# The head's modulation: weights in whole rows, transpositions for one-column products, small tables on GpSimd's queue

## What is computed

```python
cond = jax.nn.silu(c)
for layer in range(DEPTH):
    mod = cond @ ada_w[layer] + ada_b[layer]
    sh_m, sc_m, gt_m, sh_f, sc_f, gt_f = jnp.split(mod, 6, axis=-1)
    h = modulate(rms_norm(x, norm_mix[layer]), sh_m, sc_m)
    ...
# modulate(hn, shift, scale) = hn * (1 + scale) + shift
```

## Time and profile before

| | us |
|---|---|
| median of 3 timed runs | 2018.76 |
| lowest and highest of them | 2018.72 and 2019.66 |
| the profiled execution | 2013.86 |
| its span, first to last instruction | 2012.0 |
| TensorE busy in it | 1691.6 |
| VectorE busy | 606.6 |
| ScalarE busy | 361.9 |
| GpSimd busy | 74.2 |

### The profile page before, as it was taken

The page is one execution under the profiler, slowest core; times in us unless marked ns, Lnnn a source line. Parts: engine busy times, 40 slices in busy tenths (PEclk is TensorE's granted clock), DMA queues, the critical chain, the costliest instruction groups (busy, mean ns, idle before and its releaser), DMA issues.

```text
span 2012.0 us, 26580 instructions
## 1 busy us (share of the span) xinstructions
PE 1691.6 (84%) x11294; PEld 1049.1 (52%) x11294; DVE 606.6 (30%) x1546; ACT 361.9 (18%) x817; POOL 74.2 (4%) x80
## 2 busy tenths in 40 slices
PE   6997879976777667999987776787799998999988
PEld 4756754533333333755544333353378874568753
DVE  1657633211111112662320111111141053311292
ACT  1113213100000001322311100010121223211271
POOL 0000100000000001000000000000100000000000
PEclk9997998988788889999888888898899999999899
DMA  9995326999999999773699999999983343066100
GB/s 352 377 310 209 85 85 255 419 428 428 428 428 429 428 428 409 268 269 123 265 426 422 427 430 428 424 427 428 421 291 139 130 168 115 1 189 201 53 1 32
DMA packets 142766, 582.33 MB, mean 289 GB/s; under 512 B 30940, under 2 KB 42332, under 8 KB 117984
## 3 DMA queue, kind: packets, MB, share of 16 engines
q1 hardware_dynamic: 113504, 558.49, 69.3%
q10 hardware_dynamic: 24000, 10.32, 2.0%
q0 software_dynamic: 5184, 12.43, 1.8%
HBM read 571.41 MB, written 13.11 MB: 291 GB/s over the span
## 4 chain that ended last, share of the span: by engine, by line
PE 50%; DMA 35%; DVE 8%; issue 2%; ACT 2%; PEld 1%; PEldq 1%; SPq 0%; DVEq 0%; ACTq 0%; POOL 0%; POOLq 0%
DMA ring<-in_exp_w_dram 31%; PE bank L735 15%; PE bank L724 6%; PE bank L872 6%; PE bank L2133 5%; PE bank L2497 3%; PE bank L2194 2%; PE bank L2487 2%; DMA ring<-in_hawk_w_mem_kv_dram 1%; PE bank L2139 1%; DMA ring<-in_ada_w_dram 1%; DMA taken_rows<-expert_out,route_rows 1%; PE bank L1999 1%; DVE pair_probs L3273 1%; DVE pair_probs L3258 1%
## 5 line engine op out<-in xcount | busy, mean ns | idle before, releaser
L2133 PE MATMUL bank<-ring,hidden_room 128*32 128x512 f32 x2032 | 291.5, 697 | 165.8 <-DMA ring<-in_exp_w_dram 163.4
L735 PE MATMUL bank<-hT,ring 128*128 128x256 f32 x1344 | 294.0, 381 | 2.6 <-ACTq L167 2.2
L735 PEld LDWEIGHTS bank<-hT,ring 128*128 128x128 f32 x1344 | 256.6, 191 | 39.1 <-issue 2.8
L2133 PEld LDWEIGHTS bank<-ring,hidden_room 128*32 128x32 f32 x2032 | 66.2, 121 | 318.9 <-DMA ring<-in_exp_w_dram 175.8
L2194 PE MATMUL bank<-ring,hidden_room 128*32 128x256 f32 x1984 | 162.4, 481 | 46.7 <-DMA ring<-in_exp_w_dram 30.9
L2394 DVE COPY hidden_room<-bank 128x512 f32<-128x512 f32 x64 | 44.3, 691 | 513.0 <-PE bank L2133 513.0
L2139 PEld LDWEIGHTS bank<-kc,hidden_room 128*128 128x128 f32 x1024 | 133.9, 204 | 73.0 <-issue 65.5
L2139 PE MATMUL bank<-kc,hidden_room 128*128 128x32 f32 x1024 | 141.3, 284 | 3.0 <-DVE hidden_room L2394 1.6
L2194 PEld LDWEIGHTS bank<-ring,hidden_room 128*32 128x32 f32 x1984 | 75.4, 131 | 100.8 <-issue 68.1
L2301 ACT COPY hidden_room<-bank 128x512 f32<-128x512 f32 x64 | 37.5, 586 | 474.8 <-PE bank L2133 474.8
L724 PE MATMUL bank<-ring,hT 128*128 128x512 f32 (+2 forms) x288 | 114.3, 557 | 0.0
(11 more groups left out here) (588 smaller groups left out, 1845.9 us busy)
## 6 DMA issues: line engine op xcount, KB each, us to landing
ring<-in_exp_w_dram SPq DMA_DIRECT2D x189, 2048.0 KB, 26.6
ring<-in_ada_w_dram SPq DMA_DIRECT2D x24, 2048.0 KB, 16.8
ring<-in_hawk_w_in_dram SPq DMA_DIRECT2D x15, 2048.0 KB, 9.2
ring<-in_even_w_in_dram SPq DMA_DIRECT2D x7, 2048.0 KB
ring<-in_gla_w_in_dram SPq DMA_DIRECT2D x6, 2048.0 KB, 20.2
ring<-in_nsa_w_in_dram SPq DMA_DIRECT2D x5, 2048.0 KB, 8.2
ring<-in_even_w_out_dram SPq DMA_DIRECT2D x2, 2048.0 KB
expert_out<-kc POOLq DMA_DIRECT2D x8, 512.0 KB, 9.2
```

What stands on the lines that cost most here:

```text
L735: last = nc.tensor.matmul(pair[m // 2][0:rows, (m % 2) * T:(m % 2 + 1) * T], w[:, k, m * P:m * P + rows], src[:, k, :], start=(k == 0), st ...
L2133: last = nc.tensor.matmul(dst[quarters[k % NQ], :], own[:, q, k % 2, k // 2, :], w[:, k, :], start=(k < NQ), stop=(k >= KD - NQ))
```

## The change

Chunks 0 to 3 keep their 2 MB but are cut the other way: chunk q now holds two blocks of 128 rows of ada_w and all 2048 columns, so that a partition reads two runs of 8 KB. With that each chunk adds to all four banks (condition_rows), and the sums are ready only after the fourth. turn_tiles moves behind the fourth chunk. The one-column products give way to four times four transpositions of 128 columns (turn_row_parts), after which VectorE adds the four partial sums with a reduction for each bank. ScalarE copies two banks, VectorE the two others. The 14 small tables are issued by GpSimd at the start of the stage in place of ScalarE. The loads of c, x, first_gain and ada_bias by ScalarE stay as they are and in their order. The last keep_warm has four products in place of three and waits for the first reduction.

```diff
@@ chunk list
-                for j in range(4):
-                    ada_chunk(0, j)
+                for q in range(4):
+                    cols_of(A["ada_w"][0], 2 * q, 2, [(0, 2048)])
@@ new functions
+        def condition_rows(c, q, dsts, cond):
             for j in range(4):
+                for n in range(2):
+                    g = 2 * ((j + q) % 2) + n
+                    last = nc.tensor.matmul(dsts[j][32 * g:32 * g + 32, :], cond[:, 2 * q + n, :], slot(c)[:, n, 512 * j:512 * (j + 1)],
+                                            start=(q < 2), stop=(2 <= q))
+            return last
...
+        def turn_row_parts(dst, parts, j):
+            for m in range(4):
+                last = nc.tensor.transpose(dst[:, m * P:(m + 1) * P], parts[:, j, m * P:(m + 1) * P], ident)
             return last
@@ ScalarE
-                        for stage_rows, table in ((rowsB, COL_B), (rowsA, COL_A)):
-                            for name, (at, n) in table.items():
-                                act.dma_start(stage_rows[at:at + n, :], flat(A[name]).rearrange("(r p) -> r p", p=P)).then_inc(tables_in.up(16), 16)
-                        for j in range(4):
-                            act.wait_ge(chunk_used.sem, used0 + j + 1)
+                        act.wait_ge(chunk_used.sem, used0 + 4)
+                        for j in (0, 1):
                             nc.scalar.copy(parts[:, j, :], bank[4 + j][:, :]).then_inc(parts_copied.up(), 1)
...
+                    @block.gpsimd
+                    def _(pool):
+                        for stage_rows, table in ((rowsB, COL_B), (rowsA, COL_A)):
+                            for name, (at, n) in table.items():
+                                pool.dma_start(stage_rows[at:at + n, :], flat(A[name]).rearrange("(r p) -> r p", p=P)).then_inc(tables_in.up(16), 16)
@@ VectorE
-                        dve.wait_ge(picked.sem, picked.at(1))
+                        dve.wait_ge(chunk_used.sem, used0 + 4)
+                        for j in (2, 3):
+                            nc.vector.tensor_copy(parts[:, j, :], bank[4 + j][:, :]).then_inc(vector_steps.up(), 1)
+                            other_parts[j] = vector_steps.n
                         dve.wait_ge(bias_in.sem, bias_in.at(32))
-                        nc.vector.tensor_tensor(mod[0][:, 1, :], bank[4][:, 0:KD], ada_bias[:, 0, 0, :], ALU.add)
-                        nc.vector.tensor_tensor(mod[0][:, 0, :], bank[4][:, KD:2 * KD], ada_bias[:, 0, 1, :], ALU.add).then_inc(vector_steps.up(), 1)
+                        for n, j in enumerate((0, 2, 1, 3)):
+                            dve.wait_ge(picked.sem, picked.at(n + 1))
+                            four = bank[4 + j][:, :].rearrange("p (m g r) -> p m g r", m=4, g=4)[:, :, :, 0]
+                            nc.vector.tensor_reduce(row_sums[:, 4 * j:4 * j + 4], four, AX.X, ALU.add).then_inc(vector_steps.up(), 1)
+                            other_parts.setdefault("first sum", vector_steps.n)
+                        dve.wait_ge(vector_steps.sem, vector_steps.n)
+                        nc.vector.tensor_tensor(mod[0][:, 1, :], row_sums[:, 0:KD], ada_bias[:, 0, 0, :], ALU.add)
+                        nc.vector.tensor_tensor(mod[0][:, 0, :], row_sums[:, KD:2 * KD], ada_bias[:, 0, 1, :], ALU.add).then_inc(vector_steps.up(), 1)
@@ TensorE
-                        for j in range(4):
-                            if j == 3:
-                                pe.wait_ge(consts_in.sem, consts_in.at(16))
-                                pe.wait_ge(normed.sem, normed.at(TT))
-                                turn_tiles(pe, xn, turned)
-                            arrived(pe, c0 + j)
-                            condition_products(c0 + j, bank[4 + j], cond).then_inc(chunk_used.up(), 1)
-                            if j == 0:
+                        for q in range(4):
+                            arrived(pe, c0 + q)
+                            condition_rows(c0 + q, q, bank[4:8], cond).then_inc(chunk_used.up(), 1)
+                            if q == 0:
                                 pe.wait_ge(consts_in.sem, consts_in.at(16))
-                            if j < 3:
+                            if q < 3:
                                 keep_warm(bank[0], 4)
-                        pe.wait_ge(parts_copied.sem, parts_copied.at(4))
-                        sum_row_parts(bank[4], parts).then_inc(picked.up(), 1)
-                        keep_warm(bank[5], 3)
+                        pe.wait_ge(normed.sem, normed.at(TT))
+                        turn_tiles(pe, xn, turned)
+                        for n in range(2):
+                            pe.wait_ge(parts_copied.sem, parts_copied.at(n + 1))
+                            turn_row_parts(bank[4 + n], parts, n).then_inc(picked.up(), 1)
+                            pe.wait_ge(vector_steps.sem, other_parts[n + 2])
+                            turn_row_parts(bank[6 + n], parts, n + 2).then_inc(picked.up(), 1)
+                        pe.wait_ge(vector_steps.sem, other_parts["first sum"])
+                        keep_warm(bank[4], 4)
```

More of the change, by code:

```diff
@@ L445, in condition_products, with sum_row_parts @@
             return last
-        def sum_row_parts(dst, parts):
+        def condition_rows(c, q, dsts, cond):
             for j in range(4):
+                for n in range(2):
[3 more added lines that the diff above has]
+            return last
+        def sum_row_parts(dst, parts, which=range(4)):
+            for j in which:
                 for m in range(4):
                     last = nc.tensor.matmul(dst[:, 4 * j + m:4 * j + m + 1], parts[:, j, m * P:(m + 1) * P], pick, start=True, stop=True)
+            return last
+        def turn_row_parts(dst, parts, j):
+            for m in range(4):
+                last = nc.tensor.transpose(dst[:, m * P:(m + 1) * P], parts[:, j, m * P:(m + 1) * P], ident)
             return last
@@ L462, in head_stage @@
                 parts = sb(st, "mod_parts", [P, 4, 512])
+                row_sums = sb(st, "mod_row_sums", [P, 2 * KD])
                 c_in, x_in = signal("vector_in"), signal("operands_in")
@@ L468, in head_stage @@
                 used0 = chunk_used.n
+                other_parts = {}
                 with Stage(whole, met) as block:
```

## The result

| | before | after |
|---|---|---|
| median of 20 timed runs each, in us | 2018.24 | 2023.82 |
| lowest and highest | 2012.44 and 2025.3 | 2020.57 and 2027.41 |
| span of the profiled execution | 2012.0 | 2019.0 |

What follows compares the result with a forecast made beforehand. The head's chain to the first projection (L735) was taken to bound the kernel; a late ada_bias moves that start to 48.7 - 40.15 = +8.5 us, and 2018.76 + 8.5 = 2027.3. Range 2020 to 2030.5 (0.82), own case 2023.5 to 2030.5.

Steps and rivals of the forecast that it cites:

- a turn is a row of memory, whatever its length: DMA queues q1 and q10: they alternate row by row, so one 4-byte element passes for each weight row, even of 8 KB.
- The table was put at 44.5 us: Landing of ada_bias, which VectorE awaits before the first reduction: 28.4 + 16.1 = 44.5 us, between 43 and 46.
- first rival: Head's small tables: several elements go in one turn, bias in time, first projection at 37.6, -2.6 us, 2016.2; chance 0.10.
- second rival: First chunks' DMA: 8 KB rows go in two turns of 4 KB, bias at 38.3, +2.4 us, 2021.1; chance 0.05.
- Fourth chunk: Last of the head's first weight chunks: arrives at 27.3 us, 3.5 us earlier, through longer rows and fewer small turns.
- row parts turned: Head's tail on TensorE: products, turn_tiles and 16 transpositions done by 33.1 us, hidden behind the wait for the bias.
- first projection: Start of L735 behind the head: at 48.7 us in place of 40.15, after the bias and 3.6 us of work.
- c came at 3.8 us and not at 7: Load of c on ScalarE's queue: its last 185 elements, 12 turns of about 0.35 us, end at about 7, not 3.7.
- its own case: Whole kernel: the late bias delays the first projection, +8.5 us to 2027.3, held at 2023.5 to 2030.5; chance 0.78.
- third rival: Stages behind the head: the late start is partly given back by VectorE's work and the full ring, 2021 to 2025; chance 0.04.
- a microsecond there is a microsecond of the whole: Start of L735: it moves everything behind it, the experts' stream too, so its shift reaches the end whole.
- the term that I had at 8.5: First projection's new start less the old, 48.7 - 40.15 = +8.5 us, added whole to the median.

Runs made afterwards that it cites:

- rows4k: Changed kernel with each of the four first weight chunks loaded by two DMAs of 1024 columns, rows of 4 KB: +1.0 us against before (-1.2 to 3.0).
- rows2k: Changed kernel with each of the four first weight chunks loaded by four DMAs of 512 columns, rows of 2 KB: -2.8 us against before (-4.6 to -0.8).
- delay3: Kernel before with 6 added keep_warm products at the end of the head: first projection 4.6 us later, whole +12.5 us (8.3 to 16.8).
- delay8: Kernel before with 17 added keep_warm products at the end of the head: first projection 9.5 us later, whole +4.6 us (2.4 to 6.7).
- rowbias_late: rowbias with 8 more keep_warm products at the end of the head: first projection at 38.57 us, whole 1.4 us faster than before (-3.6 to 0.8).
- rowbias_again: rowbias unchanged, run again with more rounds: first projection at 37.18 us, whole -8.1 us against before (-11.3 to -4.6).
- rowbias: Changed kernel with first_gain and ada_bias loaded as 24 rows of 512 bytes and transposed once, not 3072 single elements: -9.1 us against before (-12.3 to -5.7).

## Why the prediction was right, and where its size was off

**The queue, right.** The step that gave the sign was that a turn is a row of memory, whatever its length. The table was put at 44.5 us and its landing is at 44.51; the queues were put at about 810 packets each and show 789 and 786; rows4k and rows2k move the landing as the rule says, to within 2 us. The first rival, several elements in one turn, is out. The rule of the Trainium skill (DMA: Bandwidth & Descriptors, section Queues, rings and completion order), that an engine drains typically 9 to 17 descriptors before it turns, stood beside it. The prediction held the equal counts against that rule, but they alone don't speak against it, since drains of equal length in both rings give equal counts too. The 16 and 16 packets in 0.32 us do: here the turn is one descriptor. The second rival (8 KB in two turns, table at 38.3) is out as well: that is about where rows4k lies (39.7), which really has twice the rows. The 4096 bytes that the prediction quotes from the Trainium skill (DMA: Bandwidth & Descriptors, section SWDGE vs HWDGE vs iDMA) stand there in a table on the DMAs that GpSimd issues, and these rows were SyncE's, so they lent that rival nothing.

**The head, right in sum and nearly so in its parts.** Fourth chunk 28.16 (27.3 was put), row parts turned 33.72 (33.1), ScalarE held by the issue of ada_bias until 10.1 (10), x at 14.1 (15), four reductions 0.42 us in all (0.7), eight keep_warm records 3.42 (3.6), first projection 48.56 (48.7). c came at 3.8 us and not at 7. The prediction gave its last elements one turn for each row of 8 KB, but from 3.0 to 3.4 us q10 has 149 packets beside 11 of q1: at the very start the queues did not yet go one for one. Nothing hung on it.

**The carrying, wrong in size.** The time came out at 2023.82 us, just inside the 2023.5 to 2030.5 that the prediction held for its own case and just as well inside the 2021 to 2025 of its third rival. The step that failed is the sentence "a microsecond there is a microsecond of the whole". It rested on the chain alone, which showed no wait for weights between 40 and 383 us. The chain was right on that, and 8.1 of the 8.4 us were still whole at line 724 (91.6 in place of 83.5). But the work behind it does not keep its length when it is moved. By line 1300 the changed kernel was 12.8 us late, at the experts' first product (line 2133) 11.6 against the first profile of the kernel before but 7.1 against its second, and at the end 5.0 by the timings, so 3.5 us less than the term that I had at 8.5. The rise to 12.8 is shown: pure delays have it too, with the granted clock beside it for 3.4 of its 4.7 us. The fall back is not settled. The two profiles of each kernel place 2 to 4 us of it between lines 1405 and 713 (the changed kernel 82.6 and 82.7 us, the kernel before 84.8 and 86.3), and the rest, by the difference to the timings, behind the start of the experts, where the profiles of one and the same kernel differ by up to 3 us in a stretch (292.8 and 295.6 from line 2380 to line 1999 in the kernel before). My third rival had said that the milestone would not carry, and gave it 0.04, with the reason that VectorE's slack and the full ring would give it back. What the runs show is that the work behind changes its length with its start, in both directions: from 4.6 us lost for 9.5 to 12.5 lost for 4.6. With such a spread for pure delays, the 8.4 us of this start could as well have ended outside the forecast's range. That they ended within it is in part luck; that the first projection came within 0.2 us of its forecast is not.

## What to carry to other kernels

When a load's rows are made longer, look at what else is in flight in another queue: a table of single elements gets one of them for each row beside it, so that 3072 elements of 4 bytes, harmless next to rows of 2 KB, became the last thing of the head next to rows of 8 KB. Load such a table as rows and turn it with one transposition: with that one edit the changed kernel's first projection came 12 us earlier, and the whole went from 5 us slower to 8 to 9 us faster than the kernel before. Of that gain the head accounts only for the 3 to 3.6 us by which the first projection then beats the kernel before: with the same edit and a start 1.4 to 2.0 us later only 1.4 us (-0.8 to 3.6) were left. And where the granted clock depends on when small products come, do not expect a local gain of a few microseconds to reach the end one to one; make the same kernel start a little later as a control before you believe either sign.

## What the runs showed of the hardware that I had not expected

- A shift of all that follows the head by 1.4 to 17.4 us, without any other change to its work, changed its time by amounts between -5 and +8 us beyond the shift (delay3 +12.5 for 4.6, delay8 +4.6 for 9.5, rowbias_late 6.7 slower than rowbias_again for 1.4 later, all by the centres of intervals that are 4 to 8 us wide).
- The dip of the granted clock behind a run of one-column products came at the same places in both profiled executions of the changed kernel, and in neither of the kernel before. But it is not fixed for one program: rowbias had it behind the first run and rowbias_again, 0.6 us later, behind the second.
- TensorE stood still for 4.44 us between two transpositions, waiting for nothing that the profile shows, in a program that had six products more than the kernel before some 770 us earlier. A pause of 2.38 us of that kind stands in the kernel before too, at 1301 us.
- The single elements go fast when they are alone: 839 of them were through by 3.0 us, against 2780 in 16 us beside rows of 2 KB. In the changed kernel, 696 packets of q10 passed from 2.6 to 3.0 us.
